# Modulation and gate sums two attention units sooner in a hybrid attention and PEER decoder layer

## The reference, cut to what matters

```python
mod = c_act @ w_ada[l] + b_ada[l]
sh1, sc1, g1, sh2, sc2, g2 = jnp.split(mod, 6, axis=-1)
h = rmsnorm(x, norm1_g[l]) * (1.0 + sc1[:, None]) + sh1[:, None]
proj = h @ w_in[l]
dq, dk, dv, mq, mk, mv = jnp.split(proj, splits, axis=-1)
d_out = diff_attention(...)      # 4 heads, two softmax maps each, per-head RMS norm
m_out = moba_attention(...)      # 8 heads; 256 positions are one block, so plain causal
mix = jnp.concatenate([d_out, m_out], axis=-1) @ w_out[l]
x = x + g1[:, None] * mix
h2 = rmsnorm(x, norm2_g[l]) * (1.0 + sc2[:, None]) + sh2[:, None]
x = x + g2[:, None] * peer(h2, peer_wq[l], peer_keys[l], peer_u[l], peer_v[l])
return rmsnorm(x, final_g)
```

## Time and profile before

| | us |
|---|---|
| median of 3 runs | 998.0 (996.73 to 998.27) |
| the profiled execution's own time | 998.27 |
| its span | 996.5 |
| PE busy | 957.6 (96%) |
| DVE busy | 717.6 (72%) |
| ACT busy | 454.7 (46%) |
| POOL busy | 177.1 (18%) |

### The profile page before, as it was taken

The page is one execution under the profiler, slowest core; times in us unless marked ns, Lnnn a source line. Parts: engine busy times, 40 slices in busy tenths (PEclk is TensorE's granted clock), DMA queues, the critical chain, the costliest instruction groups (busy, mean ns, idle before and its releaser), DMA issues.

```text
span 996.5 us, 16326 instructions
## 1 busy us (share of the span) xinstructions
PE 957.6 (96%) x6378; PEld 870.4 (87%) x6378; DVE 717.6 (72%) x1370; ACT 454.7 (46%) x823; POOL 177.1 (18%) x88
## 2 busy tenths in 40 slices
PE   4999997999999999999999999999999999999995
PEld 3888787999999999999999999988888888888884
DVE  4528895937999987889999995555555555555555
ACT  3133345426444534544444444544455544455553
POOL 1000100877999960000000000000000000000000
PEclk9999979999999999999999999999999999999998
DMA  8999493023555555455455455556666566665662
GB/s 330 367 414 361 201 418 151 24 106 109 189 169 178 183 168 171 150 160 157 149 157 161 149 155 181 177 191 198 196 191 190 192 194 197 198 192 190 192 192 102
DMA packets 47899, 193.13 MB, mean 194 GB/s; under 512 B 5312, under 2 KB 7504, under 8 KB 46416
## 3 DMA queue, kind: packets, MB, share of 16 engines
q1 hardware_dynamic: 47760, 192.07, 57.5%
q0 software_dynamic: 64, 0.03, 0.0%
HBM read 191.00 MB, written 1.07 MB: 193 GB/s over the span
## 4 chain that ended last, share of the span: by engine, by line
PE 87%; POOL 6%; DVE 4%; ACT 1%; issue 1%; DMA 1%; SPq 0%; DVEq 0%; ACTq 0%
PE banks L893 23%; PE banks L900 12%; PE banks L869 11%; PE banks L873 11%; PE banks L870 11%; PE banks L717 5%; POOL lo L429 4%; PE banks L884 3%; PE banks L713 3%; POOL wq_low L422 2%; PE banks L694 2%; PE banks L668 1%; PE banks L675 1%; DMA small_cols<-in_cols 1%; PE banks L700 1%
## 5 line engine op out<-in xcount | busy, mean ns | idle before, releaser
L1241 DVE TENSOR_TENSOR lo<-raw,hi 128x1024 fp32r<-128x1024 f32 x210 | 258.9, 1233 | 169.8 <-ACT hi L569 168.4
L569 ACT ACTIVATE hi<-raw 128x1024 fp32r<-128x1024 f32 x256 | 271.6, 1061 | 169.6 <-PE banks L900 169.6
L869 PE MATMUL banks<-h2r,hi 128*128 128x256 f32 x1024 | 256.4, 288 | 0.0
L893 PE MATMUL banks<-hi,wsplit 128*128 128x512 f32 x1024 | 253.1, 389 | 0.5 <-DVE wsplit L1282 0.5
L870 PE MATMUL banks<-h2r,hi 128*128 128x256 f32 x1024 | 251.0, 283 | 0.0
L893 PEld LDWEIGHTS banks<-hi,wsplit 128*128 128x128 f32 x1024 | 192.2, 188 | 40.5 <-issue 0.7
L870 PEld LDWEIGHTS banks<-h2r,hi 128*128 128x128 f32 x1024 | 196.5, 192 | 0.0
L869 PEld LDWEIGHTS banks<-h2r,hi 128*128 128x128 f32 x1024 | 196.0, 191 | 0.0
L873 PE MATMUL banks<-h2r,lo 128*128 128x256 f32 x1024 | 143.9, 283 | 3.4 <-POOL lo L429 3.4
L900 PE MATMUL banks<-lo,wsplit 128*128 128x512 f32 x512 | 137.0, 389 | 0.0
L873 PEld LDWEIGHTS banks<-h2r,lo 128*128 128x128 f32 x1024 | 132.0, 192 | 4.2 <-POOL lo L429 4.2
(11 more groups left out here) (171 smaller groups left out, 910.6 us busy)
## 6 DMA issues: line engine op xcount, KB each, us to landing
raw<-in_u_t SPq DMA_DIRECT2D x128, 512.0 KB, 3.6
raw<-in_v_b SPq DMA_DIRECT2D x128, 512.0 KB, 3.5
g_w<-in_w_gate SPq DMA_DIRECT2D x2, 4096.0 KB, 21.2
wq<-in_wq SPq DMA_DIRECT2D x2, 4096.0 KB, 18.9
sh_w<-in_w_mod SPq DMA_DIRECT2D x8, 512.0 KB, 14.3
sc_w<-in_w_mod SPq DMA_DIRECT2D x8, 512.0 KB, 14.9
win<-in_w_in SPq DMA_DIRECT2D x8, 512.0 KB, 14.6
win<-in_w_in SPq DMA_DIRECT2D x1, 4096.0 KB, 21.4
```

The costliest lines, as they stand in the source:

```text
L569: nc.scalar.activation(hi_t[:, n % HI, :], raw[n % RAW][:, :], ACT.Copy).then_inc(high_ready, 1)
L869: nc.tensor.matmul(dst, w, h2r[:, 0, c, :], start=(c == 0), stop=False)
L893: nc.tensor.matmul(bank[2 * t + half][:, :], wsplit[:, j % WS, e, t * P:(t + 1) * P], hi_t[:, n % HI, half * 512:half * 512 + 512], start= ...
L1241: nc.vector.tensor_tensor(lo_t[n % RAW][:, :], raw[n % RAW][:, :], hi_t[:, n % HI, :].bitcast(F32), ALU.subtract).then_inc(vector_low, 1)
```

## The change

The sum of sc2 begins at unit 1 and no longer at unit 3, that of g1 at unit 5 (before 7), and that of sh2 at unit 9 (before 11). All sums are over after unit 12, and units 13 and 14, which had chunks before, have none. The chunks, their order and their operands are the same. The two halves of the gate row are made by PE in units 11 and 12 (before 12 and 13). DVE reads them there, and it reads them ahead of that unit's chunks and no longer behind them.

```diff
-                if a in (LATE + 1, LATE + 2):
-                    if a == LATE + 1:
+                if a in (LATE, LATE + 1):
+                    if a == LATE:
                         pe.wait_ge(proj_out, N_IN)
                         pe.wait_ge(acc_ready, 1)
                     else:
                         pe.wait_ge(rows_read, 1)
-                    mod_row(acc, a - LATE - 1, bank[3]).then_inc(rows_ready, 1)
+                    mod_row(acc, a - LATE, bank[3]).then_inc(rows_ready, 1)
...
-                if 3 <= a < 7:
-                    mod2("sc2", sc2_w, 0, range(2 * a - 6 + n, 2 * a - 5 + n), sc2_read)
-                if 7 <= a < 11:
-                    gate_sum(acc, "g1", g1_w, range(2 * a - 14 + n, 2 * a - 13 + n))
-                if 11 <= a < 15:
-                    mod2("sh2", sh2_w, 1, range(2 * a - 22 + n, 2 * a - 21 + n), sh2_read)
+                if 1 <= a < 5:
+                    mod2("sc2", sc2_w, 0, range(2 * a - 2 + n, 2 * a - 1 + n), sc2_read)
+                if 5 <= a < 9:
+                    gate_sum(acc, "g1", g1_w, range(2 * a - 10 + n, 2 * a - 9 + n))
+                if 9 <= a < 13:
+                    mod2("sh2", sh2_w, 1, range(2 * a - 18 + n, 2 * a - 17 + n), sh2_read)
...
                 if a + 1 < UNITS:
                     logits(a + 1)
+                if a in (LATE, LATE + 1):
+                    half = a - LATE
+                    cols = slice(half * 512, (half + 1) * 512)
+                    ve.wait_ge(rows_ready, half + 1)
+                    ve.wait_ge(g1row_in, 16)
+                    nc.vector.tensor_tensor(g1b[:, cols], bank[3], g1b[:, cols], ALU.add).then_inc(rows_read, 1)
                 sums(a, 0)
...
-                if a in (LATE + 1, LATE + 2):
-                    half = a - LATE - 1
-                    cols = slice(half * 512, (half + 1) * 512)
-                    ve.wait_ge(rows_ready, half + 1)
-                    ve.wait_ge(g1row_in, 16)
-                    nc.vector.tensor_tensor(g1b[:, cols], bank[3], g1b[:, cols], ALU.add).then_inc(rows_read, 1)
```

## The result

| | before | after |
|---|---|---|
| median of 12 runs each | 997.74 us | 998.69 us |
| lowest to highest | 996.08 to 998.64 | 997.62 to 1002.28 |
| the profiled execution | 998.27 | 1000.57 |

The ratio of the paired runs is 1.0018, 95% interval 1.001 to 1.0026: 1.8 us slower by the ratio (0.95 by the two medians), within the 0.2% that was called no change. A second set of the same kernel, on another chip, gave 1.0008 (0.9999 to 1.0016). The changed kernel has a tail of long runs: of its 23 runs in the two sets six took 999.9 us or more, of the kernel before none did in any set.

The account below looks back on a forecast made before the run. PE was taken to bound the attention up to unit 10, DVE from unit 12's logits. Front 2.3 us later minus tail 1.8 sooner gave 0.5 us later, 998.5 us on the median's scale; 8-in-10 range 996.5 to 1000.6.

Parts of the forecast that it names:

- front: Start of unit 1's fill to start of unit 12's logits: 2.3 us later, bounds 0.5 to 3.3.
- tail: Start of unit 12's logits to end of unit 15's maximum: 1.8 us sooner, bounds -2.0 to -1.1.
- The wait for sc2a: Unit 1: DVE waits 1.7 us for the load landing at 72.7; PE's transposes come 1.9 us late, at 75.0.
- The chunks ahead of `combine`: Units 1 and 2: chunks delay PE, 0.15 us in unit 1 without the load wait, 0.4 in unit 2.
- The clock behind the attention: From 131 us: changed idle times may shift PE's 1.2 GHz stretch, making the time 1000.5 or 997.3 us.
- slower one: Rival behind the attention: low clock lasts longer into the output product, 1000.5 us and above; chance 0.15.
- faster one: Rival behind the attention: PE keeps its clock as its gap shrinks, 0.5 to 1.7 us less, 997.3; chance 0.10.
- g1: Behind unit 6's maximum: load lands 90.8, wanted 91.7, no wait; if sc2a cost nothing, DVE would wait 1.4 us.
- POOL beside L982: Units 8 to 10: sh2 chunk blocked by POOL's instruction; 1.5 us lost costs nothing, 2.6 lost costs 0.5.
- The wait for the first row: Behind unit 12's logits: DVE waits 0.6 us, between 0.4 and 0.8, for PE's first gate-row half.
- a pair of chunks: From unit 12's logits to unit 15's maximum: DVE does two pairs instead of three, 2.4 us less.
- The queues and the rest: Load and POOL queues: sh2b issued about 5 us sooner, other loads same or sooner, POOL's unmoved; price 0.

Follow-up runs that it names:

- loads alone: Kernel before with only two loads reordered (sc2a ahead of win2, second bias table behind g1): 997.23 us, ratio 0.9997.
- rows alone: Kernel before with only the gate rows moved (PE makes them in units 11 and 12, DVE reads them ahead of the chunks): 998.51 us, ratio 1.0008.
- changed, second profile: Changed kernel once more, no edit, on another chip: median 998.24 us, ratio 1.0008; the profiled execution took 998.40 us.
- changed, sc2a first: Changed kernel with the load of sc2a issued ahead of that of win2: 996.97 us, ratio 0.9993.
- changed, both loads reordered: Changed kernel with sc2a loaded ahead of win2 and the second bias table loaded behind g1: 996.36 us, ratio 0.9988.
- sums and both loads, rows left: Kernel before with sums moved, sc2a ahead of win2, second bias behind g1; gate rows left in units 12 and 13 behind the chunks: 996.56 us, ratio 0.9991.
- changed, both loads, read behind the chunk: Changed kernel, sc2a ahead of win2, second bias behind g1, DVE's gate-row reads put behind the first chunk in units 11 and 12: 995.80 us, ratio 0.9981.
- the pair with sc2a last: Changed kernel with sc2a loaded behind sc2b: 1005.51 us, ratio 1.0087; the same with six useless PE matmuls before unit 1's transposes: 1003.16 us, ratio 1.0058.

## Why the prediction was right, and where it was not

The time (998.69, forecast 998.5) and the sign were as forecast, and so was the mechanism: a wait at the front, partly paid back by a shorter tail. That the number is so close is in part luck. The median of the kernel before was 997.74 in this set and not the 998.0 that the forecast started from, and the difference was 0.95 us by the medians, 1.8 by the ratio and 0.8 by that of the second set, where the sum had 0.5. Front and tail, in us, in the profiles:

| kernel | front | tail |
|---|---|---|
| before | 47.37 | 14.06 |
| loads alone | 47.37 | 14.07 |
| rows alone | 47.36 | 14.78 |
| changed, first profile | 52.07 | 12.37 |
| changed, second profile | 49.43 | 12.36 |
| changed, sc2a first | 48.12 | 12.36 |
| changed, both loads reordered | 47.94 | 12.36 |
| sums and both loads, rows left | 47.93 | 13.46 |
| changed, both loads, read behind the chunk | 47.95 | 11.66 |

Where DVE waits for no load, the front repeats to 0.02 us: 47.36 to 47.37 with the sums where they were, 47.93 to 47.95 with them moved. What is longer than that is the wait and what follows from it. Forecast was 2.3 us more front and 1.8 less tail; the first profile has 4.70 and 1.69, the second 2.06 and 1.70. The maximum of unit 15, forecast to end near 131.6, ended at 132.99 and at 130.86. Step by step:

- **The wait for sc2a.** The mechanism was right. The transposes of unit 1 came at 75.04, forecast 75.0, as the load landed at 72.6 again. But that agreement is of the load alone: the projection ended 1.1 us sooner in that execution (the transposes of unit 0 at 67.60 and not 68.68), so DVE waited 2.69 us and not 1.7. In two other profiles of the same order it waited 1.40 and 0.28. DMA and PE reach this point each in its own time, and the cost is their difference.
- **The chunks ahead of `combine`.** With no wait for the load the forecast left 0.15 us for unit 1 and 0.4 for unit 2, 0.55 together. The front without waits is 0.57 longer than before (47.94 against 47.37). In the second set's profile unit 2 is 0.34 us longer from fill to fill (75.49 to 80.35, before 74.31 to 78.83).
- **The clock.** This is the term that the sum lacked. I priced the low clock only behind the attention, although the wait that I put into unit 1 is an idle time of PE as well. In the first profile the fill of unit 2 took 5.31 us instead of 3.62. Of these 1.7 us some 1.3 were lost, as the 0.34 of the chunk lies under the longer fill (unit 2 is 1.68 longer in all). It does not come in each execution: it was there behind an idle time of 2.81 us, and not behind 1.52. One of the six long runs is the profiled one, with the slow fill. The other five have no trace, but a mean granted clock: four of the six have 0.984, and neither the other 17 runs of the changed kernel nor any run of the kernel before in the later sets is under 0.986. So the clock goes with the length in four of the six; the other two (1000.20 and 1000.45, at 0.986) stay unexplained. That the idle time brings the low clock is supported by the pair with sc2a last, but not proved: its one trace with the useless matmuls still has a slow fill.
- **The clock behind the attention.** Of the two rivals there, no slower one was seen: from 131 to 140 us the granted clock was 0.50 before and 0.50 after, from 140 to 165 it was 0.99 and 0.97. The faster one was seen in part, in other kernels: with sc2a first the clock was 0.89 from 131 to 140, and from the last maximum to the output product it took 7.77 us instead of 8.70. So up to 0.9 us between two single profiles can come from there, and their total times do not rank the kernels. From the output product to the end of the span it was 856.5 to 857.3 us in every profile.
- **g1.** No wait in the changed kernel, as forecast; once the first wait was gone it appeared (0.72 us), as the forecast said it would.
- **POOL beside L982.** The chunk beside POOL's instruction took 2.90 us against 1.28: 1.6 lost, where L956 had lost 1.5. DVE was idle for 0.73 us before the logits of unit 12, so it cost nothing, as forecast. This is what the Trainium skill ("SBUF — State Buffer", section "Who interferes with whom") says of instructions with two SBUF inputs.
- **The tail.** Forecast 1.8 us shorter, measured 1.69. The wait for the first row was 0.61, forecast 0.6. The split between the parts did not come out as forecast, where a pair of chunks was worth 2.4 whatever the rows do, and the rows' move cost 0.6. By the profiles: neither moved 14.06, rows alone 14.78, sums alone 13.46, both 12.37. The rows' move costs 0.7 alone and gives 1.1 where the sums have moved. DVE's two waits for PE (0.85 and 0.77 us) make up that difference, and by the estimate above they are mostly the low clock in that one execution. Whether the split is wrong at full clock stays open.
- **The queues and the rest.** No sign of a cost was seen; no run tests them by themselves.

## What to carry to other kernels

Before work that waits for a load is moved to an earlier place, subtract the two times, landing and need, and ask who else is queued behind the waiting instruction; where the load can be issued sooner at no cost, move it with the work. A wait that makes TensorE idle costs its own length and may cost more in the work behind it, at the lower clock (here 1.3 us behind 2.81 us of idle time in one execution, nothing behind 1.52 in another); price both at the place of the wait, and give the wait as a range. To compare variants that differ by less than the executions do, measure each stretch between two events of one trace, and not at absolute times. Two moves of one change need not add up, so test them in all four combinations, and look at the clock in each before you explain what is left.

## What the runs showed of the hardware

In dense work the granted clock of TensorE fell to 1.2 GHz behind an idle time of 2.81 us, when the engine was already busy again, and the 16 matmuls there took 5.31 us instead of 3.62. Behind 1.52 us, in another execution, it did not fall. With a few matmuls without use in a long wait three of four runs were about 2 us shorter (median 1003.16 against 1005.51 us), at a higher mean clock; the fourth was not. DVE's wait for the load varied by 2.4 us between executions of the same order of loads (2.69, 1.40 and 0.28 us), though each of the loads took 24.0 to 24.3 us from issue to landing: what varies is when the issue and PE's stage come, each against the other. Beside a POOL instruction of 2.61 us, a DVE multiply-and-reduce of 128x1024 took 2.90 us instead of 1.28.
